# Latent attention of a two-block model: value products by head pairs with the values stationary, row maximum by banks, output channel-major

## What is computed

```
def _attend_dense(q, k, v):
    s = jnp.einsum('bqhd,bkhd->bhqk', q, k, preferred_element_type=jnp.float32) * (QK_DIM ** -0.5)
    pr = jax.nn.softmax(s, axis=-1).astype(v.dtype)
    return jnp.einsum('bhqk,bkhd->bqhd', pr, v)

def _merge(p, attn_o, four_o, w_o_attn, w_fourier, w_out):
    ga = jax.nn.sigmoid(p[..., OFF_GA:OFF_GB])
    gb = jax.nn.sigmoid(p[..., OFF_GB:N_IN])
    return (ga * (attn_o @ w_o_attn) + gb * (four_o @ w_fourier)) @ w_out
```

## Time and profile before

| what | us |
|---|---|
| median of 3 runs (lowest, highest) | 3268.19 (3264.91, 3271.1) |
| the profiled execution, its own time | 3267.67 |
| its span, first to last instruction | 3265.8 |
| PE busy over the span | 2868.1 (88%) |
| DVE busy | 1520.2 (47%) |
| ACT busy | 1085.4 (33%) |
| mean granted TensorE clock | 0.935 |
| value products L2487, 1280 passes, busy | 150.0 |

### The profile page before, as it was taken

How to read it: one execution, slowest core, us unless ns; L and a number is a source line. 1 busy time by engine, 2 the same in 40 slices (tenths; PEclk the granted TensorE clock), 3 DMA queues, 4 the chain that set the end, 5 groups by cost and what they waited for, 6 DMA issues and landing times. The chain is left out here.

```text
span 3265.8 us, 40365 instructions
## 1 busy us (share of the span) xinstructions
PE 2868.1 (88%) x16398; PEld 2370.6 (73%) x16398; DVE 1520.2 (47%) x2028; ACT 1085.4 (33%) x1892; POOL 293.8 (9%) x304
## 2 busy tenths in 40 slices
PE   5999998998988988973897999988999989919997
PEld 4777777776778887872775878747999977817776
DVE  3225544333625224136534121026555553589997
ACT  4213311111215214141235111114555521207776
POOL 0004400000100000000100000003000000101333
PEclk9999999999999998995998799999999999859999
DMA  6554642120311112017433022210000054229998
GB/s 175 193 176 142 198 131 64 61 80 26 121 40 52 33 42 69 7 58 207 126 102 93 20 61 84 88 58 8 1 1 1 1 171 133 105 87 335 372 381 273
DMA packets 272227, 357.41 MB, mean 109 GB/s; under 512 B 54987, under 2 KB 185059, under 8 KB 270380
## 3 DMA queue, kind: packets, MB, share of 16 engines
q1 hardware_dynamic: 228908, 214.15, 20.6%
q0 software_dynamic: 31616, 119.71, 11.3%
q10 hardware_dynamic: 11520, 20.98, 1.7%
HBM read 282.70 MB, written 76.80 MB: 110 GB/s over the span
## 5 line engine op out<-in xcount | busy, mean ns | idle before, releaser
L225 PE MATMUL ps<-h_hi,st_w_lo 128*128 128x512 f32 x592 | 248.8, 420 | 15.4 <-PEq L828 9.6
L222 DVE TENSOR_TENSOR ew_lo<-wraw,ew_hi 128x1024 fp32r<-128x1024 f32 x192 | 247.0, 1338 | 18.5 <-ACT ew_hi L219 17.2
L222 DVE TENSOR_TENSOR w_lo<-wraw,w_hi 128x1024 fp32r<-128x1024 f32 (+2 forms) x116 | 120.0, 1053 | 276.8 <-ACT w_hi L219 276.1
L227 PE MATMUL ps<-h_hi,st_w_hi 128*128 128x512 f32 x592 | 234.4, 396 | 0.0
L226 PE MATMUL ps<-h_lo,st_w_hi 128*128 128x512 f32 x592 | 233.0, 394 | 0.0
L219 ACT ACTIVATE ew_hi<-wraw 128x1024 fp32r<-128x1024 f32 x192 | 196.8, 1060 | 57.6 <-DMA wraw<-w_e_up 45.1
L219 ACT ACTIVATE w_hi<-wraw 128x1024 fp32r<-128x1024 f32 (+2 forms) x116 | 104.0, 916 | 287.9 <-PE ps L227 159.8
L225 PE MATMUL ps<-w_hi,merged_lo 128*128 128x512 f32 (+2 forms) x408 | 160.5, 393 | 33.3 <-DVE w_lo L222 31.0
L225 PE MATMUL ps<-h_hi,w_lo 128*128 128x512 f32 x384 | 156.7, 408 | 19.1 <-DVE w_lo L222 19.1
L225 PE MATMUL ps<-merged_hi,w_lo 128*128 128x512 f32 x400 | 160.5, 401 | 9.8 <-DVE w_lo L222 9.8
L226 PE MATMUL ps<-merged_lo,w_hi 128*128 128x512 f32 x400 | 159.7, 399 | 0.0
(11 more groups left out here) (485 smaller groups left out, 6478.5 us busy)
## 6 DMA issues: line engine op xcount, KB each, us to landing
wraw<-w_in SPq DMA_DIRECT2D x98, 512.0 KB, 4.8
wraw<-w_e_gate SPq DMA_DIRECT2D x64, 512.0 KB, 8.6
wraw<-w_e_up SPq DMA_DIRECT2D x64, 512.0 KB, 7.7
wraw<-w_e_down SPq DMA_DIRECT2D x64, 512.0 KB, 9.8
mod_w<-w_mod POOLq DMA_DIRECT2D x12, 2048.0 KB, 9.6
gates<-st_zo ACTq DMA_DIRECT2D x48, 256.0 KB, 2.0
rw_in<-rw_scan POOLq DMA_DIRECT2D x8, 1280.0 KB, 6.5
mg_gates<-gates POOLq DMA_DIRECT2D x16, 512.0 KB, 4.8
```

The source lines that it names most:

```text
L222: return dve.tensor_tensor(dst, src, hi.bitcast(F32), ALU.subtract)
L225: pe.matmul(out, a[1], b[0], start=first, stop=False)
L227: return pe.matmul(out, a[0], b[0], start=False, stop=last)
```

## The change

Four things change in the attention stage, and one in the block behind.

- **Order**: `its` walks over pairs of heads 2c and 2c + 1, for each tile the two heads in turn. Five pieces of each head of the next pair stand in steps 2 to 11 of the 16 steps of a pair of heads; ten pieces stand ahead of the loop. Keys and queries of four heads lie in `merged`, one query in a tile of its own (`mla_q3`); `pr` lies in `wraw`.
- **Value products** for a pair of steps p, in step 2p + 2: the values of a head are stationary (64 columns), `pT` moves (128 columns). The two heads write partitions 0 to 63 and 64 to 127 of bank 2. `pT` has three buffers.
- **Inverse sums**: DVE inverts two columns (`factor`), TensorE spreads each over 64 channels (the column broadcast as the stationary operand, the identity moving), DVE copies the result to `rden` and multiplies.
- **Row maximum**: each bank is reduced as soon as its three matmuls are done, and the three are joined.
- **Output** lies channel-major in `ao`, so the block behind has no transposes and splits it in four pieces of 1024 columns.

```diff
-                its = [(h, t) for h in range(HEADS) for t in range(NT)]
+                its = [(2 * c + a, t) for c in range(HEADS // 2) for t in range(NT) for a in range(2)]
...
-                out_bank = lambda n: ps[:, 3 * ((n + 1) % 2) + 2, 256:256 + VD]
+                out_bank = lambda a: ps[64 * a:64 * a + 64, 2, 256:256 + P]
+                den_bank = lambda a: ps[64 * a:64 * a + 64, 2, 384:384 + P]
...
-                    return (h + 1, t - 1) if 1 <= t <= 5 and h + 1 < HEADS else None
+                    c, j = divmod(n, 2 * NT)
+                    return divmod(10 * (c + 1) + j - 2, 5) if 2 <= j < 12 and c + 1 < HEADS // 2 else None
...
+                        for i, (k0, w) in enumerate(CH):
+                            if i == 2 and n >= 4 and n % 2 == 0:
+                                pe.wait_ge(S("ml_o"), n // 2 - 1)
+                            products(pe, ps[:, 3 * (n % 2) + i, 0:w], q_of(h, slice(t * P, (t + 1) * P)),
+                                     k_of(h, slice(k0, k0 + w)), True, True).then_inc(S("ml_s"), 1)
...
-                    def output(n):
-                        h = its[n][0]
-                        pe.wait_ge(S("ml_pd"), n + 1)
-                        pe.wait_ge(S("ml_pa"), 2 * n + 2)
+                    def output(p):
+                        h = its[2 * p][0]
+                        pe.wait_ge(S("ml_pd"), 2 * p + 2)
+                        pe.wait_ge(S("ml_pa"), 4 * p + 4)
                         for k in range(NKT):
-                            mm = pe.matmul(out_bank(n), pT[:, n % 2, k, :], vb[:, k, h, :],
-                                           start=(k == 0), stop=(k == NKT - 1))
+                            for a in range(2):
+                                pe.matmul(out_bank(a), vb[:, k, h + a, :], pT[:, (2 * p + a) % 3, k, :],
+                                          start=(k == 0), stop=(k == NKT - 1))
+                        pe.wait_ge(S("ml_den"), p + 1)
+                        for a in range(2):
+                            mm = pe.matmul(den_bank(a), den[:, 2 * p + a:2 * p + a + 1].to_broadcast([P, HD]), ident[:, :],
+                                           start=True, stop=True)
                         mm.then_inc(S("ml_pv"), 1)
...
-                        if n:
-                            output(n - 1)
+                        if n >= 2 and n % 2 == 0:
+                            output(n // 2 - 1)
...
                     def row_max(n):
-                        dve.wait_ge(S("ml_s"), n + 1)
-                        link(dve.tensor_reduce(nm[:, n:n + 1], s3(n), X, ALU.max))
                         h, t = its[n]
-                        dve.tensor_scalar(nm[:, n:n + 1], nm[:, n:n + 1], rsq[:, 1, t, h:h + 1], None, ALU.mult
+                        part = lambda i: pm[:, n % 2, i:i + 1]
+                        for i, (k0, w) in enumerate(CH):
+                            dve.wait_ge(S("ml_s"), 3 * n + i + 1)
+                            ins = dve.tensor_reduce(part(i), ps[:, 3 * (n % 2) + i, 0:w], X, ALU.max)
+                            if i:
+                                link(ins)
+                                if i == 1:
+                                    dve.tensor_tensor(part(0), part(0), part(1), ALU.max)
+                        dve.tensor_scalar(nm[:, n:n + 1], part(2), part(0), rsq[:, 1, t, h:h + 1], ALU.max, ALU.mult
                                           ).then_inc(S("ml_m"), 1)
...
+                    def factor(p):
+                        dve.wait_ge(S("ml_e"), 2 * p + 2)
+                        dve.reciprocal(den[:, 2 * p:2 * p + 2], den[:, 2 * p:2 * p + 2]).then_inc(S("ml_den"), 1)
...
+                        dve.wait_ge(S("ml_pv"), p + 1)
+                        link(dve.tensor_copy(rden[:, :], ps[:, 2, 384:384 + P]))
+                        dve.tensor_tensor(ao[:, c, t * P:(t + 1) * P], ps[:, 2, 256:256 + P], rden[:, :], ALU.mult
                                           ).then_inc(S("ml_o"), 1)
```

More of the change, by code:

```diff
@@ L2416, in second @@
             with ExitStack() as st:
[L2417 to L2420, removed]
+                flat = tuple(h[:, :, :].rearrange("p k t -> p (k t)") for h in merged)
+                q3 = pair(st, "mla_q3", [QKD, T])
+                pr = wraw[:, :, :].rearrange("p a t -> p (a t)")[:, 0:2 * NKEY].rearrange("p (a b) -> p a b", a=2)
@@ L2427, in second, with k_of @@
                 GR = [(0, 4), (4, 4), (8, 2)]
                 N = len(its)
+                CH = [(0, 512), (512, 512), (1024, 256)]
                 s3 = lambda n: ps[:, 3 * (n % 2):3 * (n % 2) + 3, :].rearrange("p a b -> p (a b)")[:, 0:NKEY]
-                out_bank = lambda n: ps[:, 3 * ((n + 1) % 2) + 2, 256:256 + VD]
+                out_bank = lambda a: ps[64 * a:64 * a + 64, 2, 256:256 + P]
+                den_bank = lambda a: ps[64 * a:64 * a + 64, 2, 384:384 + P]
+                def k_of(h, cols):
+                    return tuple(f[0:QKD, NKEY * (h % 4) + cols.start:NKEY * (h % 4) + cols.stop] for f in flat)
@@ L2435, in head_group, with q_of @@
+                def q_of(h, cols):
+                    if h % 4 == 3:
+                        return tuple(f[:, cols] for f in q3)
+                    o = 4 * NKEY + T * (h % 4)
+                    return tuple(f[0:QKD, o + cols.start:o + cols.stop] for f in flat)
                 def head_group(h, i):
-                    src, dst, t0, n_ = (q, qT, 4 * i, NT) if i < 2 else (kb, kT, 4 * (i - 2), NKT)
-                    return src, t0, min(4, n_ - t0), dst
+                    src, of_, t0, n_ = (q, q_of, 4 * i, NT) if i < 2 else (kb, k_of, 4 * (i - 2), NKT)
+                    w = min(4, n_ - t0)
+                    return src, t0, w, of_(h, slice(t0 * P, (t0 + w) * P))
@@ L2441, in head_bank @@
                 def head_bank(h, i):
-                    return 7 if h else 7 - i
+                    n = 5 * h + i
+                    return 7 if n >= 10 else 7 - n % 8
                 def next_head(n):
-                    h, t = its[n]
-                    return (h + 1, t - 1) if 1 <= t <= 5 and h + 1 < HEADS else None
+                    c, j = divmod(n, 2 * NT)
+                    return divmod(10 * (c + 1) + j - 2, 5) if 2 <= j < 12 and c + 1 < HEADS // 2 else None
                 @block.tensor
@@ L2462, in scores @@
                         if t == 0:
-                            pe.wait_ge(S("ml_hlo"), 5 * h + 5)
+                            pe.wait_ge(S("ml_hlo"), 5 * h + 5 if h > 1 else 10)
                         if n >= 2:
                             pe.wait_ge(S("ml_e"), n - 1)
[L2466 to L2473, removed]
+                        for i, (k0, w) in enumerate(CH):
[3 more added lines that the diff above has]
+                                     k_of(h, slice(k0, k0 + w)), True, True).then_inc(S("ml_s"), 1)
                     def transposes(n, i):
@@ L2512, in _ @@
                             head(*next_head(n))
-                    output(N - 1)
+                    output(N // 2 - 1)
                 @block.scalar
@@ L2527, in probs @@
                         act.wait_ge(S("ml_t"), 3 * n + i + 1)
-                        if i == 0 and n >= 2:
-                            act.wait_ge(S("ml_pv"), n - 1)
-                        act.activation(pT[:, n % 2, g0:g0 + w, :].rearrange("p k t -> p (k t)"), ps[:, 6, 0:w * P],
+                        if i == 0 and n >= 3:
+                            act.wait_ge(S("ml_pv"), (n - 3) // 2 + 1)
+                        act.activation(pT[:, n % 3, g0:g0 + w, :].rearrange("p k t -> p (k t)"), ps[:, 6, 0:w * P],
                                        ACT.Copy).then_inc(S("ml_pa"), 1)
@@ L2535, in head @@
                         act.wait_ge(S("ml_htr"), 5 * h + i + 1)
-                        act.activation(dst[0][:, h % 2, t0 * P:(t0 + w) * P], ps[0:QKD, head_bank(h, i), 0:w * P], ACT.Copy,
+                        act.activation(dst[0], ps[0:QKD, head_bank(h, i), 0:w * P], ACT.Copy,
                                        scale=gcol[:, int(i >= 2):int(i >= 2) + 1]).then_inc(S("ml_hev"), 1)
-                    for i in range(5):
-                        head(0, i)
+                    for i in range(10):
+                        head(i // 5, i % 5)
                     exponentials(0)
```

68 lines of the change are left out of this document (28 added, 40 removed).

## The result

| | before | after |
|---|---|---|
| median us (lowest, highest, runs) | 3266.55 (3264.01, 3271.1, 4) | 3247.26 (3245.99, 3252.33, 4) |
| ratio after / before | | 0.9936 [0.992, 0.9951] |
| profiled execution, its span | 3267.67, 3265.8 | 3252.33, 3250.2 |
| attention stage, first transpose to the end of the last value or inverse-sum pass | 349.1 | 328.2 |
| value passes, busy | 150.0 | 76.9 |

The change is 19.3 us faster by the medians; 18.3 were forecast.

The account below looks back on a forecast made before the run. TensorE bounds the attention stage (busy 346 of 351 us). Plain pairs -20.7, pairs with pieces +1.5, start +4.0, pieces gone -2.2, end +0.6, next block -1.5: -18.3 from 3267.67, forecast 3249.4 us, range 3241 to 3258.

Parts of the forecast that it names:

- The value products: Attention stage: two heads' half-array passes run at once, 0.055 us a pass, 2.2 us a pair in place of 4.34.
- plain pairs: Pairs of steps without pieces of a coming head: 8.84 us each, 1.22 less than before; 17 of them give -20.7.
- Rival 1: Value products: the halves do not run at once, a pass costs 0.1085 us, 3326 us in all; chance 0.08.
- Entry and exit, inverse sums: TensorE, per pair: 0.23 us for entering and leaving the half-width form, 0.22 us for four inverse-sum passes.
- Odd steps: No value products cover ACT's copy out of bank 6 there, so TensorE waits 0.47 us in each odd step.
- the exponentials stay off the path there: Odd steps, maxima by banks: DVE and ACT need 2.3 us after the last score matmul, TensorE has 3.3.
- Pairs with pieces: Steps also transposing pieces of a coming head: DVE and ACT chain through bank 7, 11.28 us against 11.10, +0.1 a pair.
- Rival 2: Pairs with pieces: the chain is looser and they gain as plain ones do, 20 us more, 3230 us; chance 0.18.
- Maxima: DVE's row maximum by banks: 0.69 us over 512 columns, 0.42 over 256; one maximum would make 2.3 us 3.4.
- Start and end: Attention stage: ten pieces instead of five ahead of the loop +4.0 us, fewer pieces inside it -2.2, last pair +0.6.
- The block behind: Block after attention: 32 transposes go, the output is split in four pieces, -1.5 us unless the Fourier reload delays it.
- The sum: Whole kernel: all terms together -18.3 us, forecast 3249.4 us.

Follow-up runs that it names:

- Experiment 1: Changed kernel with a pair's value products one head after the other instead of in turn: 3301.03 us, ratio 1.0098.
- experiment 5: Changed kernel with the third group of transposes of an odd step moved behind the first three score matmuls of the next scores: 3247.98 us, ratio 0.9925.
- experiments 6 and 7: Pieces of later heads left out of the loop: changed kernel 3211.32 us (ratio 0.9818), kernel before 3246.85 us (ratio 0.9932).
- Experiment 8: Changed kernel with both pieces of a pair in its even step, one amid the value products, none in odd steps: 3240.71 us, ratio 0.9904.
- experiment 2: Changed kernel with one row maximum over 1280 columns after the last score matmul, as before the change: 3260.11 us, ratio 0.9973.
- experiment 3: Kernel before with only the row maximum taken bank by bank: 3268.7 us, ratio 0.9994.
- the repeated comparison: Changed kernel, unaltered, measured again beside the kernel before: 3248.04 us against 3271.59, ratio 0.9921.
- 4: Changed kernel without the inverse-sum matmuls of a pair, the wait for the inverse and DVE's extra copy and product, output unscaled: 3242.03 us, ratio 0.9912.

## Why the prediction was right

**The value products.** Right, with its size: 0.055 a pass from rows 4, 0.055 measured, and plain pairs lose 1.20 (1.22 forecast). 17 of them give 20.4 us against 20.7. Rival 1 is excluded by after's own rows. Experiment 1 confirms its price for a pass (0.109 where one half runs alone, 0.1085 in the prediction); it measured 3301 and not 3326 because five of the 44 passes still found one of the other half beside them, and because the wait for the residual rows (below) was 4.9 us there against 11.3 in after. By the Trainium skill, "TensorE: Matmul & The Clock Gate", Part 3, a load overlaps running matmuls only if its row group differs; both halves use all rows and overlap, so the measurement decides against it here. In rival 1 the two streams stand for "10 us in a row"; that is a slip, by after's rows it is 2.4.

**Entry and exit, inverse sums.** Forecast 0.23 and 0.22 a pair; 0.24 read in after, and 0.21 measured by taking the sums away.

**Odd steps.** The wait was forecast as 0.47 and is 0.41. The step of the prediction was right in size but half of the cause: taking this wait away gives nothing (experiment 5), as the third copy behind the exponential closes a round of the same length. The text says that "the exponentials stay off the path there"; the exponential lies on that round. The prediction let it start 0.71 us behind the last score matmul (0.42 + 0.04 + 0.21 + 0.04), as if only the last bank's maximum were left; DVE was still at the second bank's (until 2567.52), and the exponential starts 1.41 us behind the transposes that follow that matmul. The third copy isn't in that sum. That the pair still came out at 8.86 against 8.84 is luck in so far as this second limit happened to be no longer than the first.

**Pairs with pieces.** 11.28 forecast for a 4 + 4 pair, 11.27 measured; its two parts were off by 0.10 and 0.09 in opposite directions (5.30 for 5.20, 5.98 for 6.07), so that the sum is this near is luck. Over the 15 pairs the mean is 11.04 after and 11.0 before, +0.7 us in all where the sum had +1.5. That the pieces eat the gain of their pairs is shown by experiments 6 and 7, not by reading alone. Rival 2 was wrong for the order as given: the chain through ACT and DVE is as tight as worked out. Experiment 8 shows that in another order 0.7 us of a pair come back (10.0 us over 15).

**Maxima.** DVE's 512-wide maximum takes 0.68 and the 256-wide one 0.42, as taken from the neighbours in rows 5. That maxima by banks are worth 11.7 us of the stage is shown (experiment 2). The prediction's numbers, 3.4 us against 3.3, had one maximum cost 0.1 us in an odd step; it cost 0.57 in a plain pair, because the round over bank 6 had no slack.

**Start and end.** From the first transpose of a piece to the first score matmul, in the timelines of TensorE in before and in after:

```profile
2267.78 1.92 PE L2457 MATMUL ps<-ident,mla_q 128*96 128x128 f32 x8 [7.63 <-PEq L303]
...
2273.35 0.50 PE L225 MATMUL ps<-merged_hi,merged_lo 96*128 96x512 f32 x1 [1.52 <-DVE merged_lo L2558]
```

```profile
2269.21 1.91 PE L2471 MATMUL ps<-ident,mla_q 128*96 128x128 f32 x8 [5.94 <-PEq L303]
...
2277.99 0.50 PE L225 MATMUL ps<-merged_hi,merged_lo 96*128 96x512 f32 x1 [2.40 <-DVE merged_lo L2573]
```

That is 5.57 and 8.78: +3.2, +4.0 forecast. The five pieces that left the loop stood in steps of 5.55 us (four) and 5.26, which without them are 5.03: -2.3 (-2.2 forecast). The end is -0.2 (+0.6 forecast). These terms add up to -20.4 + 0.7 + 3.2 - 2.3 - 0.2 = -19.0; the stage is 20.85 shorter, so there are -1.8 us that no term had. They are what maxima by banks give ahead of the first output: experiment 3 has the same 1.78 us there on the kernel before, with no other part of the change, and from that kernel's stage (347.2) to after's (328.2) it is the 19.0 of the terms. About a third of it is the shorter maximum itself; the rest lies where before ran at the lower clock.

**The block behind.** From the last pass of the stage to the first merge matmul 14.16 us before and 13.77 after, -0.4, where -1.5 was forecast. This is the mis-sized term. The timeline of after in this block:

```profile
2599.46 4.63 DVE L222 TENSOR_TENSOR oa_lo<-fT,oa_hi 128x1024 fp32r<-128x1024 f32 x4 [1.39 <-ACT oa_hi L219]
...
2603.20 1.06 ACT L219 ACTIVATE of_hi<-four_raw 128x1024 fp32r<-128x1024 f32 x1 [0.93 <-DMA four_raw<-fourier]
...
2604.29 5.13 DVE L222 TENSOR_TENSOR of_lo<-four_raw,of_hi 128x1024 fp32r<-128x1024 f32 x4 [0.20 <-ACT of_hi L219]
```

The first low part starts 2.0 us after the last pass of the stage instead of 1.7, and the eight take 9.96 (2599.46 to 2609.42) instead of 9.24: ACT now reaches the Fourier part before its reload has landed and waits for it 0.93 us, and a little for each of its next pieces. The prediction had named this reload as what could hold it up.

**The sum.** Stage and block behind are 21.2 us shorter in the profiled executions, 18.3 forecast; the medians differ by 19.3 and in the repeated comparison by 23.6. The profiled executions themselves differ by 15.3 only. The stage began 1.4 us later, and behind it DVE waits for the reload of the residual rows, before and after:

```profile
2745.10 0.69 DVE L2686 TENSOR_TENSOR g_prod<-ps,g1r 128x512 f32<-128x512 f32 x1 [6.59 <-DMA x_sum<-x_rows]
```

```profile
2729.87 0.69 DVE L2701 TENSOR_TENSOR g_prod<-ps,g1r 128x512 f32<-128x512 f32 x1 [11.34 <-DMA x_sum<-x_rows]
```

That wait is longer by 4.8 us here. In the nine profiles of the experiments it lies between 4.9 and 11.8 with the changed stage (experiment 1 the shortest, 4 the longest; 10.8 in the change once more) and is 5.0 and 8.4 with the old one. Whether the change makes it longer stays open.

## What to carry to other kernels

Two independent products of at most 64 result channels can share TensorE's columns, and then the order of issue decides: in turn they cost half, one head after the other the same work costs 53 us more here. Before counting a saving of the busiest engine, work out for each kind of step the round through the other engines and the shared banks, with every instruction that stands in it; here some 54 us less of TensorE's own work, by the prediction's sum, became 19 us, and two limits of one length stood in the odd step, so that removing one alone showed nothing. A part of a change that measures as next to nothing alone (the maxima by banks) can be what the rest lives on, so test it in the changed kernel as well, and look at the start of a stage apart from its steady part.

## What the runs showed of the hardware that I had not expected

- A float32 pass with 64 stationary and 128 moving columns takes 0.109 us if only its own half is at work, as long as a pass at full width; two halves at once give 0.055 a pass. In experiment 1 sixteen of the twenty passes of the first half ran alone, although those of the second were issued right behind them.
- The two halves don't keep one order of starts: in experiment 1 a pass of the first half starts 0.10 us ahead of a pass of the second half that was issued before it. The same part of the Trainium skill says that matmuls start and end in the order of issue; these records don't agree, and whether ends keep the order wasn't looked at.
- At the stage's first step a delay of 0.6 us came to cost 1.8: TensorE's granted clock fell to the lower level behind an idle stretch of 1.64 us, and did not behind one of 1.08 us at the same place.
